# A two-block transformer kernel: start without a barrier, bias copies moved to a later stage, first heads loaded one stage earlier

## The reference

```python
# first block
xn = rms_norm(x, norm_g)                              # 1024 x 1024
qa, ka, va, za, qb, kb, vb, zb = split(xn @ w_in)     # eight parts of 512 columns
qa, ka, qb, kb = rms_norm of each head, with a gain
# 4 differential heads: bias by t5 bucket of key - query
bias = t5_bias[t5_bucket(kpos - qpos)]
a = softmax(q1 k1 / 8 + bias) - lam * softmax(q2 k2 / 8 + bias)
ya = rms_norm(a @ va, subln_g) * (1 - lam_init) * silu(za)
# 8 neighbourhood heads on a 16 x 64 grid, window 8 x 16, bias rpb by offset
yb = softmax(qb kb / 8 + rpb[dr, dc], masked) @ vb * silu(zb)
x = x + concat(ya, yb) @ w_out;  x = x + sigmoid(x @ w_gate) * (p @ w_proj)
# second block, twice, each modulated by silu(c) @ w_mod + b_mod
x = x + gate * (concat(dilated_attention, latent_attention) @ w_out_2)
x = x + gate * mlp(...)
```

## Time and profile before

| | us |
|---|---|
| median of 3 runs | 4240.02 (4237.3 to 4242.52) |
| the profiled execution | 4249.0 |
| its span, first to last instruction | 4247.2 |
| PE busy (matmul) | 3845.7, 91% of the span |
| PE weight load busy | 3210.4, 76% |
| DVE / ACT / POOL busy | 2101.1 / 1529.5 / 1650.4 |
| chain that ended last: PE | 69% |
| mean granted TensorE clock | 0.96 |

### The profile page before, as it was taken

One profiled execution on the slowest core, in us unless ns is written; L12 is line 12 of the kernel. 1 busy time (PEld: TensorE's weight loads), 2 busy tenths in 40 slices (PEclk: granted clock), 3 DMA queues, 4 the chain that ended last, 5 costly groups with the idle time before them and its releaser, 6 DMA issues.

```text
span 4247.2 us, 52791 instructions
## 1 busy us (share of the span) xinstructions
PE 3845.7 (91%) x19336; PEld 3210.4 (76%) x19336; DVE 2101.1 (49%) x3607; ACT 1529.5 (36%) x2777; POOL 1650.4 (39%) x1426
## 2 busy tenths in 40 slices
PE   2899796998789798998999999889899998999999
PEld 1788675876678687877888888777778877888887
DVE  2445285832466576744445443465567733333333
ACT  1212175732233475642221221333566632222221
POOL 2524034732454450024444444453540025444442
PEclk8999898999999899999999999899899999999999
DMA  7567344631245533222223322245522121111111
GB/s 168 159 197 212 105 124 89 125 112 62 79 116 135 143 73 76 49 95 70 94 80 97 102 75 55 76 123 136 134 69 66 43 95 60 50 50 40 60 40 55
DMA packets 285833, 402.33 MB, mean 95 GB/s; under 512 B 43876, under 2 KB 206820, under 8 KB 285028
## 3 DMA queue, kind: packets, MB, share of 16 engines
q1 hardware_dynamic: 278664, 373.79, 31.6%
q10 hardware_dynamic: 6912, 25.17, 2.1%
HBM read 311.60 MB, written 96.45 MB: 96 GB/s over the span
## 4 chain that ended last, share of the span: by engine, by line
PE 69%; issue 10%; POOL 7%; DVE 5%; POOLq 2%; ACT 2%; SPq 2%; DMA 2%; DVEq 1%; ACTq 0%
PE ps L477 6%; PE ps L479 6%; PE ps L478 6%; PE ps L2308 5%; PE ps L2310 5%; PE ps L2309 5%; PE ps L2326 5%; PE ps L2328 5%; PE ps L2327 5%; PE ps L1766 3%; POOL WL L426 2%; POOL rs L839 2%; PE ps L1461 2%; PE ps L1451 1%; PE ps L1452 1%
## 5 line engine op out<-in xcount | busy, mean ns | idle before, releaser
L426 POOL TENSOR_TENSOR WL<-RAW,WH 128x1024 fp32r<-128x1024 f32 x226 | 554.8, 2469 | 739.5 <-ACT WH L408 729.2
L477 PE MATMUL ps<-WH,XTh 128*128 128x512 f32 (+1 forms) x1536 | 616.6, 401 | 61.0 <-POOL WL L426 35.8
L478 PE MATMUL ps<-WH,XTl 128*128 128x512 f32 (+1 forms) x1536 | 604.1, 393 | 0.0
L479 PE MATMUL ps<-WL,XTh 128*128 128x512 f32 (+1 forms) x1536 | 604.0, 393 | 0.0
L408 ACT ACTIVATE WH<-RAW 128x1024 fp32r<-128x1024 f32 x226 | 233.7, 1057 | 800.8 <-PE ps L2328 362.7
L2348 DVE TENSOR_TENSOR X<-ps,X 128x512 f32<-128x512 f32 x512 | 349.2, 689 | 258.5 <-PE ps L2328 257.5
L2326 PE MATMUL ps<-WH,Hh 128*128 128x512 f32 x1024 | 403.1, 394 | 16.1 <-issue 11.7
L2308 PE MATMUL ps<-XTh,WH 128*128 128x512 f32 x1024 | 401.3, 392 | 14.9 <-issue 11.6
L2309 PE MATMUL ps<-XTl,WH 128*128 128x512 f32 x1024 | 399.8, 390 | 0.0
L2327 PE MATMUL ps<-WH,Hl 128*128 128x512 f32 x1024 | 399.8, 390 | 0.0
L2328 PE MATMUL ps<-WL,Hh 128*128 128x512 f32 x1024 | 399.8, 390 | 0.0
(11 more groups left out here) (257 smaller groups left out, 7823.3 us busy)
## 6 DMA issues: line engine op xcount, KB each, us to landing
RAW<-w_all SPq DMA_DIRECT2D x232, 512.0 KB, 3.5
WM<-w_mod ACTq DMA_DIRECT2D x48, 512.0 KB, 4.3
WM<-w_mod SPq DMA_DIRECT2D x48, 512.0 KB, 3.9
X<-x SPq DMA_DIRECT2D x2, 4096.0 KB, 13.7
X_d<-X SPq DMA_DIRECT2D x2, 4096.0 KB, 12.0
QSd<-QA_d SPq DMA_DIRECT2D x16, 512.0 KB, 3.6
KHd<-KA_d SPq DMA_DIRECT2D x32, 256.0 KB, 5.5
KLd<-KA_d SPq DMA_DIRECT2D x32, 256.0 KB, 6.1
```

Source lines behind the costliest of these rows:

```text
L426: e.tensor_tensor(w_low(n), w_raw(n), w_high(n).bitcast(F32), ALU.subtract).then_inc(w_ready, 1)
L477: e.matmul(bank, a, w, start=(kc == 0), stop=False)
L478: e.matmul(bank, b, w, start=False, stop=False)
L479: j = e.matmul(bank, a, l, start=False, stop=(kc == K - 1))
```

## The change

The separate preparation stage and its barrier go. X is loaded in two halves, the gains `BC` between them; ACT and DVE wait for the first half and `BC` only. SP issues the first three weight pieces next, then the small loads, the fourth piece, and then the store of `T5V` and the four copies into `T5B_d`. PE makes the four small products after the first half's transposes, into banks 4 to 7; DVE's copies and constants stand between the first half's `shift` and the second half's `scale`; ACT's functions between the second half's `squares` and `high`. DVE and ACT wait there for the store of `T5V`, because the preparation's tiles now lie where the projection's working tiles lie. The eight copies into `NAB_d` are issued in the differential stage, before the loads of head 2.

At the end of the differential stage, once head 2 has been used, SP loads `RMK` and head 0 of `na`; at the end of `dil`, once its head 6 is over, SP loads head 0 of `mla`. The layouts are rearranged so that these tiles lie in slots that are no longer in use. The clearing of `PTnh` and `PTnl` moves to POOL's fourth unit. The rotary keys of `mla` are loaded with heads 0 and 1, each counted with its head.

```diff
@@ -216,6 +216,26 @@
...
+        OH = sb("OH", [N_BUCKETS, 2 * S], c=c3)
...
+        sb("prep_rest", [P, PJ_TILES - 4 * S - 1152], c=c3)
+        T5V = sb("T5V", [H_DIFF, 2 * S], c=c3)
+        c3.close()
...
@@ -273,17 +288,21 @@
         QSn, KHn, KLn = sb("QSn", [P, 2, S], F32R, c2), sb("KHn", [P, 2, S], F32R, c2), sb("KLn", [P, 2, S], F32R, c2)
-        ZSn = sb("ZSn", [P, 2, T, P], c=c2)
+        PTnh = sb("PTnh", [P, 2, 6, 512], F32R, c2)
+        VSn, ZSn = sb("VSn", [P, 2, T, P], c=c2), sb("ZSn", [P, 2, T, P], c=c2)
+        PTnl = sb("PTnl", [P, 2, 6, 512], F32R, c2)
+        VHLn, OTn = sb("VHLn", [P, 2, T, P], F32R, c2), sb("OTn", [P, 2, 512], c=c2)
         Pn, BIn = sb("Pn", [P, 3, NA_KEYS], c=c2), sb("BIn", [P, 3, NA_KEYS], c=c2)
+        TMPn = sb("TMPn", [P, 256], c=c2)
+        sb("diff_rest", [P, 896], c=c2)
         NAB = sb("NAB", [P, 2, NA_E * GRID_W], c=c2)
         RMK = sb("RMK", [P, 3, NA_KEYS], c=c2)
-        TMPn = sb("TMPn", [P, 256], c=c2)
...
-        PTmh, PTml, VSm, VHLm, OTm = head_tiles(c2, "m", T)
+        PTmh = sb("PTmh", [P, 2, T, 512], F32R, c2)
+        Pm, VHLm = sb("Pm", [P, 2, S], c=c2), sb("VHLm", [P, 2, T, P], F32R, c2)
+        VSm, OTm = sb("VSm", [P, 2, T, P], c=c2), sb("OTm", [P, 2, 512], c=c2)
+        sb("dil_values", [P, 2 * T * P], c=c2)
         QMh, QMl = sb("QMh", [DQ, 2, S], F32R, c2), sb("QMl", [DQ, 2, S], F32R, c2)
         KMh, KMl = sb("KMh", [DQ, 2, S], F32R, c2), sb("KMl", [DQ, 2, S], F32R, c2)
-        Pm = sb("Pm", [P, 2, S], c=c2)
+        PTml = sb("PTml", [P, 2, T, 512], F32R, c2)
...
@@ -498,22 +502,35 @@
                 nm = led if led is not None else Normed(L, src, cols, None)
                 if led is None:
                     if who.key == "sp":
-                        early(who, first)
+                        early(who, first, 0, RAW_SLOTS)
+                        prepare_loads(e)
+                        early(who, first, RAW_SLOTS)
+                        prepare_bias(e)
                     if who.key == "act":
+                        e.wait_ge(x_loaded, 32)
                         nm.squares(e, 0)
                         early(who, first)
                         nm.high(e, 0, KC)
+                        e.wait_ge(x_rest, 16)
                     if who.key == "pool":
+                        prepare_identity(e)
                         nm.roots(e, 0)
                         early(who, first)
                         nm.low(e, 0, KC)
+                        e.wait_ge(PRE["ld"], 16 * N_SMALL)
                     if who.key == "dve":
+                        e.wait_ge(x_loaded, 32)
                         nm.scale(e, 0)
                         nm.shift(e, 0, KC)
+                        prepare_constants(e)
+                        e.wait_ge(x_rest, 16)
                     if who.key == "pe":
                         turned.groups(e, 0, KC)
+                        prepare_products(e)
                 if who.key == "act":
                     nm.squares(e, 1)
+                    if led is None:
+                        prepare_functions(e)
                     nm.high(e, KC, n_g)
                 if who.key == "pool":
                     nm.roots(e, 1)
...
             load_x(who)
-            prepare(who)
-            if key in ("act", "dve"):
-                e.wait_ge(x_loaded, 16)
-            barrier(who)
...
-                who.e.dma_start(X[:], A["x"].rearrange("(t p) d -> p t d", p=P)).then_inc(x_loaded, 16)
+                x = A["x"].rearrange("(t p) d -> p t d", p=P)
+                who.e.dma_start(X[:, 0:4, :], x[:, 0:4, :]).then_inc(x_loaded, 16)
+                who.e.dma_start(BC[:], A["cols1"]).then_inc(x_loaded, 16)
+                who.e.dma_start(X[:, 4:8, :], x[:, 4:8, :]).then_inc(x_rest, 16)
...
+        def prepare_loads(e):
+            q = PRE
...
+            for to, of in small:
+                e.dma_start(to, of).then_inc(q["ld"], 16)
+
+        def prepare_bias(e):
+            q = PRE
+            e.wait_ge(q["t5v"], 4)
+            e.dma_start(T5_d, T5V[:]).then_inc(q["t5st"], 16)
+            e.wait_ge(q["t5st"], 16)
...
+        def prepare_products(e):
+            q = PRE
+            e.wait_ge(q["ld"], 16 * N_SMALL)
+            for k in range(4):
+                e.matmul(ps[0:H_DIFF, 4 + k, :], T5[:], OH[:, k * 512:k * 512 + 512], start=True, stop=True).then_inc(q["t5"], 1)
+
+        def prepare_constants(e):
+            q = PRE
+            e.wait_ge(q["ld"], 16 * N_SMALL)
+            for k in range(4):
+                e.wait_ge(q["t5"], k + 1)
+                e.tensor_copy(T5V[:, k * 512:k * 512 + 512], ps[0:H_DIFF, 4 + k, :]).then_inc(q["t5v"], 1)
...
+            e.wait_ge(q["t5st"], 16)
+
+        def prepare_functions(e):
+            q = PRE
+            e.wait_ge(q["pos"], 1)
+            e.activation(lex[:], lsum[:], ACT.Exp).then_inc(q["castp"], 1)
+            e.wait_ge(q["ld"], 16 * N_SMALL)
+            e.activation(ct[:], cc[:], ACT.Tanh, scale=0.5).then_inc(q["castp"], 1)
+            e.wait_ge(q["pos"], 2)
+            e.activation(COS[:], COS[:], ACT.Sin)
+            e.activation(SIN[:], SIN[:], ACT.Sin)
+            e.wait_ge(q["t5st"], 16)
+
+        def near_bias(e):
+            q = PRE
...
@@ -1195,6 +1220,8 @@
+                    if h == 2:
+                        near_bias(e)
...
@@ -1215,6 +1242,12 @@
+                e.wait_ge(s["used"], a.c(0) + H_DIFF - 1)
+                following = Heads("na", 0, 0)
+                e.dma_start(RMK[:].rearrange("p a b -> p (a b)"), A["near_mask"]).then_inc(following.s["pos"], 16)
+                e.wait_ge(PRE["bst"], 16 * H_NA)
+                head_loads(e, following, 0)
+                value_loads(e, following, 0)
...
-                return (self.s["ld0"], self.s["ld1"])[h % 2], 16 * self.loads * (4 * self.run + h // 2 + 1)
+                rope = 2 * (self.run + 1) if self.kind == "mla" else 0
+                return (self.s["ld0"], self.s["ld1"])[h % 2], 16 * (self.loads * (4 * self.run + h // 2 + 1) + rope)
...
                 if u == 3:
+                    for t2 in range(T):
+                        n, n0, r = len(na_tiles(t2)), na_tiles(t2)[0] - 2 * (t2 // 4), t2 % 4
+                        for k in [k for k in range(6) if not n0 <= k < n0 + n]:
+                            e.memset(PTnh[:, t2 // 4, k, r * P:r * P + P].bitcast(F32), 0.0)
+                            e.memset(PTnl[:, t2 // 4, k, r * P:r * P + P].bitcast(F32), 0.0)
                     value_low(e, a, 0)
...
+        def head_loads(e, a, h):
+            s, slot = a.s, h % 2
+            ld = a.loaded(h)[0]
+            if a.kind == "mla":
+                if h < 2:
+                    e.dma_start(KMh[NOPE:DQ, slot, :].bitcast(F32), KR_d[0]).then_inc(ld, 16)
+                    e.dma_start(KMl[NOPE:DQ, slot, :].bitcast(F32), KR_d[1]).then_inc(ld, 16)
+                e.dma_start(QMh[:, slot, :].bitcast(F32), QM_d[h, 0]).then_inc(ld, 16)
...
+        def value_loads(e, a, p):
+            s = a.s
+            vld = a.v_loaded(p)[0]
+            if p >= 2:
+                e.wait_ge(s["vlo"], a.h0 + 2 * p - 2)
+            load_v(e, {"na": VB_d, "dil": VA_d, "mla": VM_d}[a.kind], p, p % 2, a.VS, vld)
...
         def heads_sp(who, a):
             e, s = who.e, a.s
-            for h in range(8):
-                slot, p = h % 2, h // 2
+            for h in range(0 if a.kind == "dil" else 1, 8):
                 if h >= 2:
...
+                head_loads(e, a, h)
...
+            if a.kind == "dil":
+                e.wait_ge(s["full"], a.u0 + 56)
+                e.wait_ge(s["vlo"], a.h0 + 6)
+                following = Heads("mla", a.run, 2 + 2 * a.run)
+                head_loads(e, following, 0)
+                value_loads(e, following, 0)
...
-            if key == "sp":
-                e.wait_ge(PRE["bst"], 16 * H_NA)
-                e.dma_start(RMK[:].rearrange("p a b -> p (a b)"), A["near_mask"]).then_inc(s["pos"], 16)
...
         def mla_attention(who, L):
-            e, key, s = who.e, who.key, AT["mla"]
-            if key == "sp":
-                for slot in range(2):
-                    e.dma_start(KMh[NOPE:DQ, slot, :].bitcast(F32), KR_d[0]).then_inc(s["pos"], 16)
-                    e.dma_start(KMl[NOPE:DQ, slot, :].bitcast(F32), KR_d[1]).then_inc(s["pos"], 16)
-            if key == "pe":
-                e.wait_ge(s["pos"], L * 64 + 64)
             heads(who, Heads("mla", L, 2 + 2 * L))
```

More of the change, by code:

```diff
@@ L332, in sems @@
             return {n: sem(f"{stage}_{n}") for n in names.split()}
+        N_SMALL = 11 + 3 * DEPTH_2
         PRE = sems("pre", "ld t5 t5v t5st tpst bst pos castp")
@@ L344, in build_program @@
         AT = {"diff": {**diff_loop, **sems("diff", "map0 map1 rest")}, "na": {**heads_all, **sems("na", loads + " bias")},
-              "dil": {**heads_all, **sems("dil", loads + " bias qc nd0 nd1 nd2")}, "mla": {**heads_all, **sems("mla", loads)}}
```

(53 more changed lines are left out.)

238 lines of the change are left out of this document (77 added, 161 removed).

## The result

| | us |
|---|---|
| changed kernel, median of 4 runs | 4149.32 (4149.27 to 4151.8) |
| kernel before, 4 runs beside it | 4241.27 (4237.3 to 4250.71) |
| ratio | 0.9781, 95% interval 0.9765 to 0.9798 |
| the profiled execution's span | 4147.5, clock 0.967 |

A forecast was written before the change was run, and what follows sets the result against it. PE was taken to set the pace from 96.6 us on, behind a chain of waits in SP's queue. Start 55.8, `na` 15.5, `mla` 11.1 and 11.0 sum to 93.4 us off 4240.0: 4146.6, range 4136 to 4162.

The forecast's parts named there:

- SP's queue: At the start: small loads take 15.3 us, fourth weight piece issued at 22.1, landed at 26.3, first tile at 41.0.
- X by halves: At the start: first half of X with `BC` lands at about 10 us; if both halves land together, at 15.4.
- First half "costs nothing": At the start: squares begin at 10, scaling ends at 18.5 us, ahead of the weights, so it costs nothing.
- The products: Before the first tile: PE's four small products, 6.98 us, fit a 7.04 us gap and cost nothing.
- DVE's constants: Between the halves: 10.4 us of constants free DVE at 51.4, scaling ends at 54.1, fitting PE's cover within 0.6 us.
- The store: At the start: store of `T5V` takes 3 us from about 41.8, over before DVE's 51.4.
- Rival 1: At the start: the store takes 10.74 us again and what stands behind it comes last; costs 3.3 us, 4149.9; chance 0.13.
- The `na` border: With head 0 preloaded, PE starts at the barrier (694.6) instead of 710.11: 15.5 us gained.
- The `mla` borders: Preloading head 0 gains 11.1 us in layer 1 (9.9 wait, 1.2 clock) and 11.0 in layer 2.
- The copies' cover: Differential stage: eight `NAB_d` copies, issued from 534 on, take 27 us while SP waits until 573.19 anyway: hidden.
- Rivals 2 to 4: Preparation between halves does not fit, 4156.6, chance 0.07; preloads gain nothing, 4184.2, 0.03; change does nothing, 4240, 0.02.
- rival 5: Stages behind the start: PE's mean granted clock falls from 0.96, making it slower; at 0.93, 4280 us; chance 0.03.

The follow-up runs named there:

- e4: Changed kernel with the eight `NAB_d` copies back in SP's queue, behind the small loads and ahead of the fourth weight piece: 4185.85 us, ratio 0.9868.
- e2: Changed kernel with the mask and head 0 of `na` loaded behind the barrier again: 4164.5 us, ratio 0.982.
- e3: Changed kernel with rope keys and head 0 of both `mla` stages loaded behind the barrier again: 4168.08 us, ratio 0.9828.
- e11: The changed kernel unchanged, profiled and timed once more: 4151.37 us, ratio 0.9792.
- e6: Changed kernel with each of PE's four table products made twice: 4154.77 us, one run.
- e7: Changed kernel with the eight near-bias copies issued ahead of head 3's loads instead of head 2's: 4152.79 us.
- e5: Changed kernel with POOL's first weight splits waiting until DVE has scaled the first half's four tiles: 4156.89 us, one run.

## Why the prediction was right, and where its terms were off

**The sum.** 55.0 us arrive at the end of the projection (443.00 against 498.04), 1.3 are lost on the way through the differential stage, and the borders give 15.5, 9.7 and 10.8: 89.7, against medians 92.0 and, in the second series, 90.4 apart. Forecast were 55.8, none lost, 15.5, 11.1 and 11.0. The 99.7 us between the two profiles are these 89.7 and 11.6 us of luck in the dilated ramps: 3.0 in layer 1, 8.6 in layer 2 (3.9 of wait and 4.7 of ramp). That makes the 101.3 us by which the two stand apart at the first `mla` product of layer 2; 1.6 are lost behind it, and where is open. Separate runs bear out some 70 of the 92 us: e4 the copies, e2 and e3 the borders.

**The start: right in the sum, by terms that were partly wrong, and with luck.** The shift of tile 0's transposition is 56.2 us between the two first profiles, against 55.8 forecast. But those were the slower of two profiles before and the quickest of six after; taking any pair, it is 52.2 to 56.2 us.
- *SP's queue.* 16.3 us for the small loads (5.68 to 22.0) instead of 15.3; fourth piece issued at 22.04, forecast 22.1; landed by 26.7, forecast 26.3; first dense product 41.37, forecast 41.0. e11 shows what this number carries: with the piece 1.5 us later, the first dense product came 1.65 us later (43.02).
- *X by halves.* ACT's first instruction was released at 10.82 (forecast 10), not at 15.4 or later, so the first half landed alone. The Trainium skill, "DMA: Bandwidth & Descriptors", section "Rules for kernel authors", speaks of halves by partitions; for these halves by tokens the trace shows no such price.
- *First half "costs nothing".* True for the end, wrong in size. ACT loads a table first (1.28 us), and the scaling took 9.00 us, not 2.74: I moved work from a place where POOL was idle to one where it splits weights. It ended at 26.97 instead of 18.5. PE's transposes and the first `NF` (28.24) followed, and ACT's first `XTh` was done at 29.66, 0.6 us before POOL was free of its fourth split (27.87 to 30.23). A cover of 8 us had shrunk to that.
- *The products.* I took 6.98 from the earlier trace rows for a gap of 7.04. They took 3.59 in one profile of the new start and up to 6.99 in the others; e6 shows that they are on the path as soon as they are longer. In e11 the granted clock beside the 6.99 is 0.50. In the kernel before, both profiles have 6.98 with a PEclk column of 1.00, so that column doesn't explain the value I took, and its cause is open. The 3.59 of the first profile was a gift, and not in the forecast.
- *DVE's constants.* 39.19 to 51.0 with the copies, and the transposes at 54.15 (forecast 54.1 to 54.5). That PE's two tiles and DVE's chain end within 0.4 us of one another was read rightly from the earlier trace rows. PE's side ended last: in e11 too the scaling was over at 55.90 and the transposes began at 56.14, with PE busy up to then.
- *The store.* 2.4 us (41.67 to 44.06), forecast 3; with the copies gone from ahead of it in the queue, the old 10.74 us did not come back. Rival 1 falls. The fifth piece was there at 67.43 without a wait.
- *Not in the forecast:* the first projection transposition was 56.2 us earlier, but DVE's `QN` of tile 2 only 55.1: PE ran at clock 0.50 behind the stall until about 79 us, 5 us behind it, where before it was back at 1.00 after 3.

**The differential stage** was not in the sum. Its first scores wait 14.24 us for `T5B` instead of 13.52 (13.32 in e11), and small steps take 0.6 us more. e7 and e4 show that the latter aren't the copies'; what they are stays open. In e11, e7, e6 and e4 a further 1.1 us is lost at the 14th of the 32 units, which the first profile did not have.

**The `na` border** was exact: 15.48 measured, 15.2 in e2. **The `mla` borders** were 20.5 us by waits and 18.8 by e3, for a forecast of 22.1. The step that failed is the clock: I added 1.2 us because PE's clock was 1.00 at the barrier, but in the changed kernel it was 0.50 behind the barrier all the same, in layer 1 even from 1530 us on, ahead of it. The rest is the 1 to 2 us by which such a wait differs from execution to execution.

**The copies' cover.** Issue took 31.9 us, not 27, in a hole that ended 7.2 us later; e7 and e4 give its price, 7 us and 36.5 us, when that cover is gone. The clearing of `PTnh` cost nothing, as forecast: POOL's wait for ACT in that unit is 1.46 us where it was 3.78. Rivals 2 to 4 fall with the trace; rival 5 as well, the mean clock rose from 0.96 to 0.967.

## What to carry to other kernels

Work that is moved into an engine's idle time takes on the neighbours of its new place: read what the other engines do there before taking its old duration (2.74 became 9.00 us). Small transfers that the next stage needs one by one belong in the queue in the order of their use; two loops swapped in `dil` gave 10 us, over a tenth of what the whole restructured start and its preloads gave. And compare two profiles only after a second one of the same kernel: here some 8 of 100 us were luck, nearly all of it in the two dilated ramps.

## What the hardware showed that was not expected

- DVE's scaling from SBUF to SBUF and POOL's subtraction alternate by whole instructions: 0.75 us alone, 2.83 us beside splits of 2.36 us (e5).
- The granted clock was 0.50 from 36 to 47 us in a stretch in which PE was busy throughout, with table products of 32 rows by 4 columns (e6). The same four products took 3.59 to 6.99 us from one profile to the next.
- DRAM-to-DRAM copies delay a 512 KB load that is issued behind them from 4.7 to 13 us, from its issue to ACT's first use (e4).
- One kernel's start differs by 2 us between executions (128.25 and 130.27 before, 74.08 to 76.10 after), and the ramp of a stage that waits for a chain of loads by up to 6 us.
